# Where SyncE issues the stores of the rotated query group in MLA's weight-expansion block

## The reference, cut to what matters

```python
q = (rms_norm(cq, q_norm) @ w_uq).reshape(B, T, N_HEADS, MLA_NOPE + MLA_ROPE)   # 384 -> 16 x (64 + 32)
kv = (ckv @ w_ukv).reshape(B, L, N_HEADS, MLA_NOPE + MLA_V)                     # 256 -> 16 x (64 + 64)
qr_l = rope_2d(qr_l, cos_r, sin_r)                                             # rotates the 32 "rope" rows
```

## Time and profile before

| | us |
|---|---|
| median of three runs | 4034.32 (4027.93 to 4036.26) |
| the profiled execution, its own time | 4037.71 |
| span of its trace | 4035.9 |
| mean granted clock of PE | 0.988 of full speed |
| the block in layer 0, turns 0 to 12 | about 251 to 321 us from the span's start |
| the block in layer 3, turns 0 to 12 | about 3132 to 3202 us |

### The profile page before, as it was taken

How to read it: one execution, slowest core, us unless ns; L and a number is a source line. 1 busy time by engine, 2 the same in 40 slices (tenths; PEclk the granted TensorE clock), 3 DMA queues, 4 the chain that set the end, 5 groups by cost and what they waited for, 6 DMA issues and landing times. The chain is left out here.

```text
span 4035.9 us, 57984 instructions
## 1 busy us (share of the span) xinstructions
PE 3893.6 (96%) x20892; PEld 1931.6 (48%) x20892; DVE 2665.9 (66%) x3536; ACT 2332.7 (58%) x3099; POOL 1132.1 (28%) x831
## 2 busy tenths in 40 slices
PE   6999999999999999999999999999999999999998
PEld 3554444444455544444445554555455444444444
DVE  6345777777457478888845427888543568777754
ACT  4433777777444358787843217888333457777762
POOL 0000343434230024454521003444210014444442
PEclk8999999999999999999999999999999999999999
DMA  6237323232102342222111324332111652212111
GB/s 241 65 102 223 92 55 77 60 72 64 60 32 76 116 113 51 65 64 62 37 66 51 108 91 117 91 90 63 62 46 70 186 151 46 55 42 55 42 38 66
DMA packets 376225, 329.42 MB, mean 82 GB/s; under 512 B 247664, under 2 KB 295344, under 8 KB 374480
## 3 DMA queue, kind: packets, MB, share of 16 engines
q1 hardware_dynamic: 376016, 326.60, 29.0%
HBM read 235.30 MB, written 91.23 MB: 81 GB/s over the span
## 5 line engine op out<-in xcount | busy, mean ns | idle before, releaser
L796 PE MATMUL bank<-H_hilo,w_hilo 128*128 128x512 f16 (+1 forms) x5760 | 1046.1, 344 | 13.6 <-DVE w_hilo L1046 10.1
L2238 ACT ACTIVATE p_f<-bank 128x1024 f32<-128x1024 f32 (+2 forms) x768 | 742.1, 966 | 485.9 <-PE bank L2184 454.6
L2184 PE MATMUL bank<-q_slots,k_slots 96*128 96x512 f16 (+7 forms) x3968 | 939.8, 366 | 6.0 <-PEq L1197 3.6
L1992 DVE TENSOR_REDUCE max_parts<-bank 128x1 f32<-128x512 f32 (+1 forms) x1248 | 799.1, 663 | 206.0 <-PE bank L1931 199.7
L2305 DVE TENSOR_TENSOR p_lo<-p_f,p_hi 128x1024 f16<-128x1024 f32 (+2 forms) x624 | 750.9, 1206 | 156.2 <-ACT p_hi L2242 151.6
L796 PEld LDWEIGHTS bank<-H_hilo,w_hilo 128*128 128x128 f16 x5760 | 563.7, 98 | 495.8 <-DVE w_hilo L1046 11.1
L2242 ACT ACTIVATE p_hi<-bank 128x1024 f16<-128x1024 f32 (+2 forms) x768 | 739.1, 962 | 0.0
L2184 PEld LDWEIGHTS bank<-q_slots,k_slots 96*128 96x128 f16 (+2 forms) x3968 | 369.7, 98 | 396.8 <-issue 27.0
L1931 PE MATMUL bank<-k_slots,q_slots 96*128 96x512 f16 (+4 forms) x1392 | 474.6, 369 | 24.9 <-DVE max_parts L1992 20.8
L2371 POOL TENSOR_TENSOR p_lo<-p_f,p_hi 128x1024 f16<-128x1024 f32 x144 | 315.6, 2192 | 567.5 <-ACT p_hi L2242 544.1
L2353 POOL TENSOR_TENSOR o_gated<-o_f,gate_rows 64x512 f32<-64x512 f32 (+1 forms) x192 | 235.5, 1226 | 778.5 <-DVE o_f L2285 571.5
(11 more groups left out here) (203 smaller groups left out, 3963.1 us busy)
## 6 DMA issues: line engine op xcount, KB each, us to landing
ada_w<-in_w_ada SPq DMA_DIRECT2D x48, 768.0 KB, 5.4
gate<-z_ring SPq DMA_DIRECT2D x32, 640.0 KB, 3.3
gate_rows<-gate SPq DMA_DIRECT2D x64, 320.0 KB, 4.0
q_slots<-q_mla SPq DMA_DIRECT2D x64, 240.0 KB, 3.2
k_mla<-H_hilo SPq DMA_DIRECT2D x64, 224.0 KB, 3.2
k_slots<-k_mla SPq DMA_DIRECT2D x64, 224.0 KB, 4.4
cq_hilo<-v_scratch SPq DMA_DIRECT2D x64, 224.0 KB, 3.3
w_f<-in_mla_in SPq DMA_DIRECT2D x24, 512.0 KB, 4.0
```

The source lines that it names most:

```text
L796: ins = pe.matmul(dst, lhs(a, k), rhs(b, k), start=(k == 0 and n == 0), stop=(k == nk - 1 and n == 2))
L1992: dve.tensor_reduce(mx[:, par, t, c:c + 1], MB[(b * NE + k) % 2][:, 0:n], AX.X, ALU.max).then_inc(s_red.h, 1)
L2184: ins = pe.matmul(dst, lhs, rhs, start=(m == 0), stop=(m == len(ops) - 1), skip_group_check=swa)
L2238: act.activation(p32[:, p % 2, 0:cols], src, ACT.Exp, scale=scale).then_inc(s_p32.h, 1)
```

## The change

In every turn SP now issues the pair's stores of the turn before (`t - 1 in turns_out`) between the turn's loads and the turn's nope store. Pair A is so issued in turn 5 behind loads 12 and 13 and ahead of nope 1, and pair B in turn 8 behind loads 18 and 19 and ahead of nope 4.

```diff
                     for n in range(LANDING, NP):
                         if pieces[n - LANDING][0] == t:
                             load(n)
+                    if t - 1 in turns_out:
+                        for item in (2 * turns_out[t - 1], 2 * turns_out[t - 1] + 1):
+                            sp.wait_ge(s_rl.h, s_rl.base + item + 1)
+                            store_item(sp, item)
                     if t in item_of:
                         sp.wait_ge(s_lo.h, s_lo.base + lows_of[t])
                         store_item(sp, item_of[t])
-                    if t in turns_out:
-                        for item in (2 * turns_out[t], 2 * turns_out[t] + 1):
-                            sp.wait_ge(s_rl.h, s_rl.base + item + 1)
-                            store_item(sp, item)
```

## The result

The changed kernel takes 4043.26 us (median of 7 runs, 4038.26 to 4048.69) where the kernel before takes 4034.32 (7 runs): ratio 1.0021, 95% interval 1.0012 to 1.0030, so slower by 5 to 12 us. Predicted were 4037.5 us in a range of 4029 to 4044. The direction held. The range held by 0.7 us only: by the ratio the change costs 8.5 us (8.9 by the medians), over two and a half times the 3.2 us forecast, and the time is nearer to the second rival's 4043.7 than to my 4037.5.

A forecast was written before the change was run, and what follows sets the result against it. PE, busy 96% of the span, bounds the kernel. Its 2.74 us hole becomes one of 3.1 us further on; values start 1.6 us late in each of two layers, 3.2 us in all: 4034.3 goes to 4037.5, range 4029 to 4044.

The forecast's parts named there:

- second rival: SP's wait ahead of pair A delays the queue; 6 us hole ahead of key 0's second unit, 4043.7 us; chance 0.14.
- Turn 5, the gain: Load 12 starts at 284.2 and lands at 287, not 292.1; ACT's 4.83 us of idle time goes, worth nothing.
- Turn 5, the price: Pair A starts at 285.5, 5.0 us later; PE gets a 1.2 us hole ahead of tile 9's second half.
- From pair A to pair B: SP's queue between the pairs' starts: 17.5 us instead of 18.1, so pair B starts at 303.0 rather than 298.62.
- Turn 8: Loads 18 and 19 land by 305.0; PE's hole ahead of tile 11's second half is 0.2 us instead of 2.74.
- Turn 11: Load 20 lands at 316.0; 3.1 us hole ahead of key 0's second unit; values start 1.6 us late, at 322.4.
- my lower bound: Turn 11, load 20 takes only 3.1 us from its issue at 311.5; hole 1.7 us, values 1.4 us early.
- The lower clock: Behind the hole ahead of key 0's second unit, PE's clock is at its lower level for a while, costing 1.6 us.
- Layer 3: Its block has the same order and the same hole, so it again costs 1.6 us.
- The first rival: Pairs drain faster; PE's holes of 2.74 and 2.33 us go with their clock loss, 8.1 us less, 4026.2; chance 0.10.

The follow-up runs named there:

- a_only: Against the kernel before, only pair A's stores moved, to turn 5 behind loads 12 and 13; pair B left in its old place; ratio 1.0027.
- q16_old: Kernel before with each pair stored to its own tensor, 128 rows in a row, and ten loads a head instead of six; ratio 1.0158.
- late_keys: Kernel before with four key pieces loaded and split from turn 14 on and the last two value pieces split a turn later; ratio 0.9990.
- `both`: Kernel before with the edits of late_keys and early_first together; ratio 0.9985.
- early_first: Kernel before with the first two heads' query loads a turn earlier and the key's rotated rows fetched once per buffer and layer; ratio 0.9990.
- pool_pair: Kernel before with all four rotated items stored by GpSimd's own queue instead of SP; ratio 0.9998.

## Why the prediction was right, and where its size was off

On the clock of before (+3.4 us), step by step in layer 0:

- **Turn 5, the gain:** load 12 started at 284.2, as said. DVE stood nowhere in turn 7 for a weight, so the 4.83 us of ACT were worth nothing. Right.
- **Turn 5, the price:** pair A started at 285.3 (285.5). ACT could write item 3 at 292.90 on the trace's own clock, 11.0 us after the pair's start (11.1; 10.3 in layer 3 and in a_only). ACT got piece 14 at 299.2 (299). The hole ahead of tile 9 was 1.32 us (1.2); in layer 3, 1.01. Right. That moving pair A is what costs is shown by a_only; its hole ahead of tile 9 is only the first part of that cost.
- **From pair A to pair B:** this is the step that failed. I put pair B's start 17.5 us after pair A's, on the ground that the number of issues between them is the same, and load 14's issue at 8.7 us. They were 301.03 - 281.86 = 19.2 and 10.2 us. Before, the two loads behind the pair took 1.5 and 1.3 us to issue, and I had let most of that queueing vanish with them. It did not: nope 1's four stores took 5.83 us to issue where they had taken 3.02. Other traces bear this out in the main: from a pair's first issue to the first load of the next turn, SP needs 10.2 to 11.1 us where two loads and a nope tile's four stores stand between (before, both layers), and 9.6 to 10.2 with the four stores alone (the change). So taking away two loads of some 3 us of issue gives back 0.1 us at this place, and 0.6 in the mean of the four pairs, where I had counted on 1.6. So pair B started at 304.4, 1.4 us later than I had it.
- **Turn 8:** load 18 landed by 306.8 (305.0) instead of 310.5, item 2 was stored 6.7 us after the pair's start (7), and nope 6 was written at 311.1 (310.0). PE's second half of tile 11 began at 313.5 (312.2), and so the 1.4 us that this step was to give back were 0.1.
- **Turn 11:** load 20 was taken at 317.2, 12.8 us after pair B's start (316.0, 13.0 after it), the hole was 3.15 us (3.1), and values started at 323.85 (322.4). It was not slow to land: it took 3.2 us from its issue, and what came late was the issue, at 314.0 behind 5.23 us for nope 4's four stores, where my lower bound had SP there at 311.5. ACT stood 4.76 us for it (3). The whole miss of 1.4 us is the term above. The lower clock came as forecast.
- **Layer 3:** I took it as equal. The change there costs 3.8 us, 0.8 more: before had lost 0.4 us less in it (A 34.7 where layer 0 has 35.1), with load 18 landing 6.9 us after its issue instead of 7.6, and the change lost 0.4 more (38.5 and 38.1), with 6.1 us of holes instead of 5.8.

Per block 3.1 and 3.8 us instead of 1.6 make 6.9. The other 1.6 us up to the measured 8.5 lie within the interval, and no run shows a place for them. So of the 5.3 us by which the forecast of the whole was short, 3.7 are in the blocks and have their steps above; that the range still held is in part luck.

The second rival's time, 4043.7, was nearly met and its mechanism was not: it wanted load 20 at 319 or later and 4.7 us a block, and load 20 was taken at 317.2. The first rival fell at a point that I hadn't named as well: q16_old, late_keys and `both` have all of PE's holes up to the values closed, 8.8 us, and at the first head's loads 2.4 to 3.1 us of it are lost again.

## What to carry to other kernels

Here four stores that kept about half of the DMA engines busy held up the loads queued right behind them, so look first at the outermost dimension of a slow store and at what an engine must take before its urgent tile, and only then at the order of issue. When a wait is moved in front of a long transfer, count all that is queued behind it: the two loads that were freed landed 5.5 us (load 12) and 3.7 us (load 18) earlier, and the queue that was set back cost more. And a hole that closes is worth only what the next wait leaves; read on to the next engine's first use of something loaded before summing.

## What was unexpected of the hardware

- SP's issue time behind the pair is set mainly by the pair: from pair A's first issue to the issue of load 14 it was 10.3 us with two loads and four stores between, 10.2 us with four stores alone, and 9.6 in a_only, which has four stores alone as well.
- Storing through GpSimd's queue did not free SP: the issue of one 128 KB load took 3.65 us where 0.6 is usual.
- A hole of 3.05 us (early_first, layer 0) was followed by 24 matmuls in 4.70 us at a granted clock of 1.00, where one of 2.74 us was followed by the same 24 in 6.07, and one of 2.45 us (pool_pair, layer 0) by 6.39 at a clock down to 0.52. The loss of clock behind a hole is not the same every time.
- Four more loads a head (q16_old) cost 62 us net over 32 heads, nearly 2 us each, of which PE's own waits for them are 49.2 us.
